# The inverse root of each norm on ScalarE as exp(-0.5 ln), its table loaded ahead

## The reference

```
x += 0.5 * post1(SwiGLU_1(pre1(x)))
x += post2(W_out concat[A, B, C, D](pre2(x)))
x += 0.5 * post3(SwiGLU_2(pre3(x)))

def rms_norm(x, g):
    y = x * rsqrt(mean(x * x, axis=-1) + 1e-6)
    return y * g
def swiglu(x, w_gate, w_up, w_down):
    return (silu(x @ w_gate) * (x @ w_up)) @ w_down
```

## Time and profile before

| | us |
|---|---|
| median of 3 runs | 1602.6 |
| lowest, highest | 1593.21, 1604.79 |
| the profiled execution | 1603.99 |
| its span | 1602.2 |

### The profile page before, as it was taken

How to read it: one execution, slowest core, us unless ns; L and a number is a source line. 1 busy time by engine, 2 the same in 40 slices (tenths; PEclk the granted TensorE clock), 3 DMA queues, 4 the chain that set the end, 5 groups by cost and what they waited for, 6 DMA issues and landing times.

```text
span 1602.2 us, 27946 instructions
## 1 busy us (share of the span) xinstructions
PE 1353.2 (84%) x9968; PEld 1257.8 (79%) x9968; DVE 944.8 (59%) x1508; ACT 652.6 (41%) x1054; POOL 216.7 (14%) x176
## 2 busy tenths in 40 slices
PE   6999979977587579999889999697866857699997
PEld 5999979966375369999889999697754735699996
DVE  4766355485654666664467654655756554666634
ACT  4655343343200255554456544434330004455543
POOL 1000010022332230000110000200323322200000
PEclk9999989967686589999989999899556966899998
DMA  6555554354461334555646556363444613255553
GB/s 213 183 184 160 163 177 131 96 155 138 147 192 49 93 105 134 184 172 162 182 129 190 172 155 181 106 199 97 129 130 138 185 38 106 83 184 183 159 168 94
DMA packets 286118, 234.15 MB, mean 146 GB/s; under 512 B 19898, under 2 KB 282018, under 8 KB 286056
## 3 DMA queue, kind: packets, MB, share of 16 engines
q1 hardware_dynamic: 286056, 233.37, 47.9%
HBM read 228.65 MB, written 5.37 MB: 146 GB/s over the span
## 4 chain that ended last, share of the span: by engine, by line
PE 76%; DVE 15%; ACT 3%; issue 3%; DMA 1%; SPq 0%; DVEq 0%; POOLq 0%; ACTq 0%
PE ps L1391 20%; PE ps L1392 19%; PE ps L1393 19%; PE ps L1590 2%; PE ps L1688 2%; DVE s L1114 2%; PE ps L1535 2%; DVE nlo L937 2%; PE ps L1687 1%; DVE yt L920 1%; PE ps L1538 1%; ACT whi L591 1%; PE ps L1504 1%; PE ps L1678 1%; PE ps L1733 1%
## 5 line engine op out<-in xcount | busy, mean ns | idle before, releaser
L1391 PE MATMUL ps<-nhi,whi 128*128 128x264 f32 x1936 | 564.2, 291 | 67.4 <-DVE nlo L937 47.0
L888 DVE TENSOR_TENSOR wlo<-raw,whi 128x1024 fp32r<-128x1024 f32 (+2 forms) x376 | 394.7, 1091 | 280.1 <-ACT whi L591 279.8
L1392 PE MATMUL ps<-nlo,whi 128*128 128x264 f32 x1936 | 558.5, 289 | 0.0
L1393 PE MATMUL ps<-nhi,wlo 128*128 128x264 f32 x1936 | 557.7, 288 | 0.0
L1391 PEld LDWEIGHTS ps<-nhi,whi 128*128 128x128 f32 x1936 | 375.2, 194 | 74.2 <-DVE nlo L937 35.9
L591 ACT ACTIVATE whi<-raw 128x1024 fp32r<-128x1024 f32 (+2 forms) x376 | 336.8, 945 | 190.9 <-PE ps L1393 113.4
L1392 PEld LDWEIGHTS ps<-nlo,whi 128*128 128x128 f32 x1936 | 375.4, 194 | 0.2
L1393 PEld LDWEIGHTS ps<-nhi,wlo 128*128 128x128 f32 x1936 | 373.2, 193 | 0.0
L1391 PE MATMUL ps<-hhi,whi 128*128 128x264 f32 x704 | 202.3, 287 | 9.1 <-DVE hlo L905 9.1
L1393 PE MATMUL ps<-hhi,wlo 128*128 128x264 f32 x704 | 201.4, 286 | 0.0
L1392 PE MATMUL ps<-hlo,whi 128*128 128x264 f32 x704 | 201.0, 286 | 0.0
(11 more groups left out here) (338 smaller groups left out, 1555.8 us busy)
## 6 DMA issues: line engine op xcount, KB each, us to landing
raw<-in_ffn_gate_dram SPq DMA_DIRECT2D x44, 1024.0 KB, 5.3
raw<-in_ffn_up_dram SPq DMA_DIRECT2D x44, 1024.0 KB, 5.4
raw<-in_ffn_down_dram SPq DMA_DIRECT2D x64, 704.0 KB, 4.5
raw<-in_w_in_dram SPq DMA_DIRECT2D x24, 1024.0 KB, 5.7
kslot<-in_cache_fox_k_dram SPq DMA_DIRECT2D x128, 128.0 KB, 2.7
vslot<-in_cache_fox_v_dram SPq DMA_DIRECT2D x128, 128.0 KB, 2.4
raw<-in_w_out_dram SPq DMA_DIRECT2D x8, 1024.0 KB, 5.1
kslot<-in_state_swa_k_dram SPq DMA_DIRECT2D x32, 128.0 KB, 2.7
```

Source lines behind the costliest of these rows:

```text
L888: tt2(wlo[s][:, a:b], raw[s][:, a:b], whi[s][:, a:b].bitcast(F32), ALU.subtract).then_inc(S(f"w_lo{s}"), 1)
L1391: mm(out, wh, hi_, start=first, stop=False)
L1392: mm(out, wh, lo_, start=False, stop=False)
L1393: return mm(out, wl, hi_, start=False, stop=last)
```

## The change

`rms_of` takes Ln of the mean and then Exp with a scale of -0.5, which gives the inverse root at once; `rsqrt_of` on VectorE keeps its wait and does nothing more. `load_table` is an Ln of one column into a new tile that nobody reads; it stands on ScalarE behind the last step of gu1 and of gu2, and so makes the build place the table's load there.

```
+        spare = place("spare", [P, 1])
...
                     def rms_of(e):
 
                         act.wait_ge(S("ss"), V("ss", e + 1))
-                        act.activation(r_post[:, :] if e % 2 else r_pre, ps[:, 7, 0:N], ACT.Sqrt, bias=C("eps")).then_inc(S("rms"), 1)
+                        r = r_post[:, :] if e % 2 else r_pre
+                        ch(act.activation(r, ps[:, 7, 0:N], ACT.Ln, bias=C("eps")))
+                        act.activation(r, r, ACT.Exp, scale=-0.5).then_inc(S("rms"), 1)
+
+                    def load_table():
+
+                        act.activation(spare[:, :], C("eps"), ACT.Ln)
...
                     gu_step(1, GU_P - 1, ("dn1", 0))
+                    load_table()
...
                     gu_step(2, GU_P - 1, ("dn2", 0))
+                    load_table()
...
                     def rsqrt_of(e):
 
-                        r = r_post[:, :] if e % 2 else r_pre
                         dve.wait_ge(S("rms"), V("rms", e + 1))
-                        ch(dve.reciprocal(r, r))
```

## The result

| | before | changed |
|---|---|---|
| median of 20 runs each, us | 1599.02 | 1589.78 |
| lowest, highest | 1589.09, 1606.67 | 1583.48, 1609.10 |
| profiled execution, span | 1603.99, 1602.2 | 1584.76, 1583.0 |

The ratio is 0.9946, with a 95% interval of 0.9927 to 0.9966. It is an estimate from the fast runs, which leaves out the run of 1609.10 us, and not the quotient of the two medians. That is no change by the bound of 1%, but clearly faster by half a per cent: 9 us where 2.7 were forecast. The profiled execution of the changed kernel is one of its quickest, and that of the kernel before one of its slower ones. So their spans differ by 19 us, and a story made from these two traces alone explains twice what there is between the medians.

The account below looks back on a forecast made before the run. TensorE was taken as the bound, 76% of the span's chain of waits. Terms -1.87 - 1.41 - 0.12 - 0.22 - 1.42 + 1.74 + 0.63 = -2.7 us, from a 1602.6 median, gave 1600 us, range 1595 to 1607.

Parts of the forecast that it names:

- The price list: At each norm: Ln 0.48, table load 1.28, Exp 0.42 us plus small gaps; new pair within 0.11 us of the old.
- a drain: Rival: ScalarE empties before each table swap, an estimated +14 us by the skill, 1600.2 by the rows; chance 0.01.
- a load that waits with Ln: Rival: at norms 2, 4 and layer 1's norm 0, five loads come on the path, +3.7, 1606.3 us; chance 0.06.
- the change does not do what it says: Rival: another table is loaded before norm 1, or the early load repeats; +0.6, 1603.2 us; chance 0.01.
- Norm 1: After a down or output product, both layers: no load ahead of Ln, the mean's matmul limits; -0.93 us each, -1.87 together.
- Norm 5 of layer 0: Load follows ScalarE's own work without idle time, so VectorE's use comes at 798.34 against 799.75: -1.41 us.
- Norm 2: Both layers: Ln's load falls into 4.73 us of idle time, 0 us; wrong if TensorE's gap is above 1.9.
- Norm 4: Both layers: Exp's load and Exp stand ahead of the silu table's load, so Silu and TensorE come 0.52 us later each.
- The gates: Both layers: exp table stays from norm 2, one load less; -0.71 us each, -1.42 together; bounds 0 and 1.28 each.
- everything here is on the path: Norms 1, 3 and 5: TensorE idles 7.49 us until the first normed tile; a us saved is a us of span.
- The clock rival: Rival: longer idle time at norms 4 and layer 1's norm 0 lengthens TensorE's half-speed stretch; +2.4, 1605 us; chance 0.13.
- The early load: Table load in the down product, under at least 3.75 us of ScalarE idle time: cost 0; without cover 1.5 each, four times.

Follow-up runs that it names:

- x9: x2's kernel with three copies of the inverse root onto itself at norm 1 of both layers, about 1.0 us each; 1597.21 us, ratio 0.9977.
- x2: The changed kernel with a one-column Sqrt behind wi's last weight split, so the gates load the exp table again; 1584.80 us, ratio 0.9905.
- x7: The kernel of x2 measured once more; 1585.51 us, ratio 0.9914.
- x5: The kernel before with two copies of the inverse root onto itself at norm 1 of both layers; 1594.26 us, ratio 0.9977.
- x6: The kernel before with four copies of the inverse root onto itself at norm 1 of both layers; 1596.97 us, ratio 0.9986.
- x13: The kernel before with VectorE's two sample-shift subtractions moved to where it waits for the attention's output products; 1597.90 us, ratio 1.0000.
- x1: The kernel before with a one-column Exp behind wi's last weight split, so the gates find their table loaded; 1593.62 us, ratio 0.9968.
- x3: The kernel before with a one-column Sqrt between the gates' Exp and Ln, two table loads more; 1590.93 us, ratio 0.9958.
- x12: The changed kernel with both load_table calls taken out; 1585.17 us, ratio 0.9908.
- x11: x2's kernel with three copies at norm 1 of both layers and five at norm 5 of layer 0; 1598.41 us, ratio 0.9978.
- x14: The changed kernel with VectorE's two sample-shift subtractions moved to where it waits for the attention's output products; 1587.50 us, ratio 0.9946.
- x15: x12's kernel with VectorE's two sample-shift subtractions moved to where it waits for the attention's output products; 1585.16 us, ratio 0.9917.
- x8: The changed kernel with eight unused products on TensorE before it waits for the gates; 1590.10 us, ratio 0.9939.

## Why the prediction was wrong

The ratio stayed inside the 1% (no change), as forecast, but the time was 1589.8 us, below the range of 1595 to 1607 and 10 us below the 1600 that was forecast. Of these 10 us, 3.6 are the start of the sum: it used a median of three runs, 1602.6, and the median of twenty is 1599.0. The prediction had allowed 4 us for that. 0.8 is in the sizes of its terms, and the other 6 in a term that it didn't have.

- **The price list was right.** Ln, load and Exp are 0.48, 1.28 and 0.42 with gaps of 0.02. The rivals of a drain and of a load that waits with Ln didn't happen (at norm 2 of layer 0 the load runs at 244.90 and Ln at 249.60, after 3.42 us of idle time), nor the one that the change does not do what it says.
- **The norms.** Norm 1: -0.95 and -0.93 (predicted -0.93). Norm 5 of layer 0: -1.53 (-1.41). Norm 5 of layer 1: -0.10 (-0.12). Norm 3: -0.11, as predicted. Norm 2: -0.10 and -0.09 (0; 1.65 is below the 1.9 at which I would have been wrong). Norm 4: +0.50 and +0.47 (+0.52). Norm 0: +0.68 and +0.61 (+0.70, +0.63).
- **The gates.** TensorE's wait fell by 1.27, the whole upper bound. But the next stage, up to the product at line 1524, which waits for VectorE, grew from 6.5 to 6.9 us: net -0.9 a layer, predicted -0.71.
- **Sum of these:** -0.95 - 0.93 - 1.53 - 0.10 - 0.22 - 0.19 + 0.97 + 0.68 + 0.61 - 1.8 = -3.5, against -2.7. The terms that were named stand, most of them to 0.1 us; the gates were 0.4 too small and norm 2 has 0.2 that were put at nothing.
- **The step that failed** is in the first part: "everything here is on the path: a us saved is a us of span", and with it the sum, in which the mixers count as unchanged behind norm 1. x9 against x2 and x7 shows it: 2.0 us at norm 1 are worth 10 to 12, and the mixers go from 326.2 and 326.1 to 328.9 and 331.6 with the same matmuls. x5 and x6 show the same with the other sign: delays that cost nothing. The kernel before has long mixers (331.8 and 338.3; in x13, without the collision, 331.7 twice), and x1, x3 and x5, which have opposite signs on the path, all came out below it (the intervals of x1 and x5 just reach 1).
- **The clock rival** looked at the right engine and the wrong place. I asked whether norm 4 would lengthen a slow stretch, took 1.7 us as its price, and didn't ask how the mixers ran; their stretch, at 0.77 and 0.76 and of 331.8 and 338.3 us for the same work twice, would have shown that they have more than one length. Norm 4 itself cost nothing beyond its 0.50: over the ten us that the prediction looked at, the granted clock is 0.84 and 0.85 behind the changed kernel's two, and was 0.85.
- **The range** took the spread of the runs shown, 1593.2 to 1604.8, as noise around the place that the sum gives. x2 and x7 show that it isn't: twelve runs within 3.7 us, where 20 of before spread over 17.6. In the profiles the spread lies in the mixers, a thing that an edit can move.
- **The early load**, which I priced at nothing and credited with -0.93 twice and -1.41, does on TensorE's idle time what was said. x12 without it is as fast (0.9908 against 0.9941 and 0.9946): in its profile the 3.1 us on the path were given back, in dn1 and in the mixers. That the pair Ln and Exp brings more to the median than its tenths of a us at each norm isn't shown either: longer gates alone (x3) brought 0.9958.

So of the 9.2 us between the medians, some 3.5 are the sum. The other 6 are what is left, and by x9 and x11, in which delays undo most of x2's gain, they lie in the mixers and their clock. x13 against x14, with the subtractions moved in both, has 10.4.

**What stays open.** What makes a place good or bad I did not settle. In some profiles one pattern goes with it: where the level rises before the idle time ahead of the product at line 1605 (as in layer 0 before, at about 370, or x9 at about 372), it falls again in it, and more slow stretches follow; where it rises only behind (x2 at 380, the changed kernel at 378), the next 17 us run at full clock. That is seen, not tested, and it doesn't hold everywhere: in layer 0 of x3 the level rises behind as well (at about 383), but is back at 0.50 by 390, with mixers of 332.2. The 0.8 us at norm 1 in x12 against the 1.0 in x9 say too that the place of norm 1 alone doesn't settle it. The Trainium skill (TensorE: Matmul & The Clock Gate, What's actually happening) says that the level follows how busy TensorE has been lately, that where it changes varies from run to run, and that the cost of the slow start is under 1% of a typical span. The rows agree with the second: the same kernel has mixers of 325.6 and 336.2 us in two profiles. They agree with the first only in part, since in the scores TensorE is busy for 5.00 of 5 us at a granted clock of 0.50. To the third they can only add that 12 us of 1600 are 0.75%; but here the cost isn't the same for two kernels, and the difference is over three times the sum of the change. Why a given kernel has its place in nearly all runs, as x2 has, no run here tells.

**The fastest.** x2 with x7 (0.9905, 0.9914), x12 (0.9908) and x15 (0.9917) can't be told apart. All their medians are below the changed kernel's (0.9946 and 0.9941), but each of their intervals overlaps with its, so that they are faster is likely and not shown. Their runs lie closer together. None has an edge that its own work explains.

## What to carry to other kernels

Price an edit by the rows of the path; here that was right to 0.8 us. But before it is credited to the time, look at the granted clock of the stop-and-go stages behind it, and at the spread of the runs: where the spread is larger than the sum, run a control that does nothing but delay (a copy onto itself), at the edited place and at one further away, and check in the trace that the delay arrives where it is meant to. Where a stage has two lengths, look for a race with GpSimd: an instruction with two SBUF inputs that comes 0.3 us too late can wait 4 us.

## What was not expected of the hardware

- TensorE stays at 1.2 GHz in the scores although it is busy for 5.00 of 5 us (x8, from 341 on; before and the changed kernel, from 350 to 360).
- A delay of 1.0 us a layer ahead of the mixers changed the time by 0.6 to 0.7% (x9 against x7 and x2); all but the 2.0 us of delay lies in the mixers, whose granted clock is 0.78 and 0.77 where it was 0.78 and 0.79.
- A subtraction of 128x72 on VectorE takes 0.22 us alone and 3.92 to 4.29 us when it starts just behind the start of GpSimd's 128x2048 product; it then ends 0.1 us behind that product.
